# Expert weights of a one-core mixture-of-experts layer laid down with neighbouring rows on one partition

## The reference: what is computed

```python
pg = softmax(t @ wg + bg);  g = argmax(pg)              # one of 4 groups
le_g = (t @ we + be) restricted to group g              # 4 experts in it
v, idx = top_k(softmax(le_g), 2);  v = v / sum(v)
comb = one_hot weights p_top * v on the 16 experts
hg = einsum('td,edf->tef', t, w_gate)                   # w_gate: 16 x 1024 x 512
hu = einsum('td,edf->tef', t, w_up)                     # w_up:   16 x 1024 x 512
hid = silu(hg) * hu * comb
out = einsum('tef,efd->td', hid, w_down)                # w_down: 16 x 512 x 1024
x = layer_norm(ALPHA * x + g2 * out)
```

## Time and profile before

| | before |
|---|---|
| median of three runs | 502.61 us (501.02 to 505.34) |
| the profiled execution: time | 503.42 us |
| the profiled execution: span, first to last instruction | 501.4 us |
| what lies around the span | 2.0 us |
| mean granted TensorE clock | 0.962 |
| TensorE matmul busy | 439.5 us (88%) |
| DMA traffic | 147.16 MB, mean 293 GB/s |

### The profile page before, as it was taken

The page is one execution under the profiler, slowest core; times in us unless marked ns, Lnnn a source line. Parts: engine busy times, 40 slices in busy tenths (PEclk is TensorE's granted clock), DMA queues, the critical chain, the costliest instruction groups (busy, mean ns, idle before and its releaser), DMA issues.

```text
span 501.4 us, 6442 instructions
## 1 busy us (share of the span) xinstructions
PE 439.5 (88%) x2370; PEld 239.4 (48%) x2370; DVE 240.5 (48%) x439; ACT 120.8 (24%) x242; POOL 56.0 (11%) x58
## 2 busy tenths in 40 slices
PE   0777999999999998899999999999999998898500
PEld 0343555556554465794554355544445544553200
DVE  2651623847734257920122343444444444246797
ACT  2300158783220226251120111111111111220100
POOL 2000015357540340000000000000000000000000
PEclk9989899999999999899999999999999999999855
DMA  8999992855999045804999999999999999996003
GB/s 317 387 386 340 341 387 78 291 213 202 353 326 338 5 156 207 308 3 151 331 396 395 356 369 395 396 394 390 392 396 395 392 391 395 394 396 251 1 1 125
DMA packets 65011, 147.16 MB, mean 293 GB/s; under 512 B 3576, under 2 KB 4408, under 8 KB 64968
## 3 DMA queue, kind: packets, MB, share of 16 engines
q1 hardware_dynamic: 63776, 143.66, 77.7%
q10 hardware_dynamic: 1032, 2.81, 1.6%
q0 software_dynamic: 160, 0.10, 0.2%
HBM read 144.99 MB, written 1.58 MB: 292 GB/s over the span
## 4 chain that ended last, share of the span: by engine, by line
PE 77%; DVE 11%; DMA 5%; issue 4%; ACT 2%; SPq 0%; ACTq 0%; DVEq 0%
PE PS L1664 18%; PE PS L1432 12%; PE PS L1702 9%; PE PS L1533 8%; PE PS L1670 5%; PE PS L1363 4%; PE PS L1737 4%; DMA ring<-in_ex_w_gate 4%; PE PS L1608 4%; PE PS L1415 2%; PE PS L1709 1%; PE PS L1466 1%; PE PS L1744 1%; DMA rowB<-in_colsB 1%; PE PS L1684 1%
## 5 line engine op out<-in xcount | busy, mean ns | idle before, releaser
L1664 PE MATMUL PS<-ring,xs 128*64 128x256 f32 x896 | 102.9, 382 | 2.2 <-DMA ring<-in_ex_w_gate 1.7
L1664 PEld LDWEIGHTS PS<-ring,xs 128*64 128x64 f32 x896 | 61.9, 137 | 38.6 <-issue 10.1
L1432 PE MATMUL PS<-hT,ring 128*128 128x388 f32 x192 | 68.7, 511 | 3.9 <-DVE hT L849 3.9
L1702 PE MATMUL PS<-ring,hTs 128*64 128x512 f32 x224 | 52.9, 615 | 1.5 <-DMA ring<-in_ex_w_down 1.0
L1170 DVE SCALAR_TENSOR_TENSOR y<-PS,comb,y 128x1024 f32<-128x1024 f32 x42 | 53.5, 1278 | 0.3 <-PE PS L1744 0.3
L1432 PEld LDWEIGHTS PS<-hT,ring 128*128 128x128 f32 x192 | 37.7, 199 | 33.0 <-issue 7.7
L694 ACT CAST yh<-PS 128x512 fp32r<-128x512 f32 x14 | 8.2, 585 | 98.5 <-PE PS L1702 58.6
L1156 DVE TENSOR_TENSOR yl<-PS,yh 128x512 fp32r<-128x512 f32 x14 | 9.7, 691 | 44.6 <-ACT yh L694 44.6
L1702 PEld LDWEIGHTS PS<-ring,hTs 128*64 128x64 f32 x224 | 15.2, 140 | 31.8 <-issue 31.7
L1363 PE MATMUL PS<-ring,cond 128*32 128x512 f32 x192 | 24.9, 635 | 0.0
L1737 PE MATMUL PS<-yh,selT 64*128 64x512 f32 x84 | 20.8, 490 | 4.5 <-DVE y L1170 2.6
(11 more groups left out here) (256 smaller groups left out, 569.6 us busy)
## 6 DMA issues: line engine op xcount, KB each, us to landing
ring<-in_ex_w_gate SPq DMA_DIRECT2D x16, 2048.0 KB, 13.5
ring<-in_ex_w_up SPq DMA_DIRECT2D x16, 2048.0 KB, 15.9
ring<-in_ex_w_down SPq DMA_DIRECT2D x16, 2048.0 KB, 14.8
ring<-in_w_ada SPq DMA_DIRECT2D x12, 2048.0 KB, 14.4
ring<-in_w_in SPq DMA_DIRECT2D x3, 2048.0 KB, 20.5
ring<-in_w_out SPq DMA_DIRECT2D x2, 2048.0 KB, 10.4
xn<-in_x_sample SPq DMA_DIRECT2D x2, 512.0 KB, 6.3
pos<-in_pos SPq DMA_DIRECT2D x2, 512.0 KB, 7.2
```

Of the source, the lines that this page charges most:

```text
L1432: mm = pe.matmul(PS[:, w % 4, 0:W], wt[:, k, (w % 4) * P:(w % 4 + 1) * P], hT[:, k, :], start=(k == 0), stop=(k == KD - 1))
L1664: mm = pe.matmul(PS[HALF * h:HALF * (h + 1), j, 0:FE // 2], x(k, HALF), w[:, k, h * (FE // 2):(h + 1) * (FE // 2)], start=(k == 0), stop=( ...
L1702: mm = pe.matmul(PS[HALF * h:HALF * (h + 1), 3, :], x, w[:, f, h * 512:(h + 1) * 512], start=(f == 0), stop=(f == KF - 1))
```

## The change

The rows of an expert's matrices are dealt out differently. In gate and up units partition `p` now holds rows `8p` to `8p + 7`, which are neighbours in DRAM: one run of 16 KB. In down units it holds rows `2p, 2p + 1` of the first 256 and of the second 256: two runs of 8 KB. Chunk `k` of a gate or up unit is now every eighth feature, beginning with `k`, so `dispatch` takes every eighth column of `h2H` and `h2L` as its stationary operand (`chunk`, a step of 32 bytes), and `turn` takes every second hidden unit (`hid_chunk`, a step of 8 bytes). The matmuls of `project_in` and `project_out` are as before.

```diff
         experts = [
-            t["ex_w_gate"][0].rearrange("e (k p) n -> p e k n", p=P),
-            t["ex_w_up"][0].rearrange("e (k p) n -> p e k n", p=P),
-            t["ex_w_down"][0].rearrange("e (k p) n -> p e k n", p=P),
+            t["ex_w_gate"][0].rearrange("e (p k) n -> p e k n", p=P),
+            t["ex_w_up"][0].rearrange("e (p k) n -> p e k n", p=P),
+            t["ex_w_down"][0].rearrange("e (h p c) n -> p e h c n", h=2, p=P),
         ]
+        def expert_view(buf, j):
+            return buf[:, :].rearrange("p (h c n) -> p h c n", h=2, n=D) if j == 2 else unit3(buf)
+
+        def chunk(v, k):
+            return v.rearrange("p (q k) -> p k q", k=KD)[:, k, :]
+
+        def hid_chunk(f):
+            return hid[:, f // 2 * (FE // 2):(f // 2 + 1) * (FE // 2)].rearrange("p (q c) -> p c q", c=2)[:, f % 2, :]
...
-                sp.dma_start(weights(v, D if j == 2 else 512), experts[j][:, e]).then_inc(ring_in[v % SLOTS], 16)
+                sp.dma_start(expert_view(ring[v % SLOTS], j), experts[j][:, e]).then_inc(ring_in[v % SLOTS], 16)
...
-                        mm = pe.matmul(PS[:, 4 + n % 4, 0:HS], part[:, i, k * P:(k + 1) * P],
+                        mm = pe.matmul(PS[:, 4 + n % 4, 0:HS], chunk(part[:, i, :], k),
...
-                        mm = pe.transpose(PS[:, 2, c * P:(c + 1) * P], hid[:, c * P:(c + 1) * P], ident)
+                        mm = pe.transpose(PS[:, 2, c * P:(c + 1) * P], hid_chunk(c), ident)
```

More of the change, by code:

```diff
@@ L415, in again @@
                 for j in range(3):
-                    sp.dma_start(unit3(ring[j], D if j == 2 else 512),
-                                 experts[j][:, bass.ds(e, 1)].rearrange("p a k n -> p (a k) n")).then_inc(s["ov_in"], 16)
+                    w = experts[j][:, bass.ds(e, 1)]
+                    sp.dma_start(expert_view(ring[j], j),
+                                 w.rearrange("p a h c n -> p (a h) c n" if j == 2 else "p a k n -> p (a k) n"))\
+                        .then_inc(s["ov_in"], 16)
             overflow(sp, most, again)
```

## The result

The changed kernel takes **506.95 us** (median of 7 runs, 506.46 to 508.91) against 502.61 us, a ratio of **1.0096** with a 95% interval of 1.0073 to 1.0118. It is slower by 4.3 us, which the interval sets apart from no change. That is just under the 1% that the prediction took as what a measurement can tell, but outside its range (498.0 to 505.3 us) and on the other side of its forecast of 499.4 us.

A forecast was written before the change was run, and what follows sets the result against it. The prediction took TensorE to bound the expert stage, with 3.25 us of waits for weights to win back. With 0 for dispatch and transposes, 502.61 - 3.25 = 499.4 us; range 498.0 to 505.3 us.

The forecast's parts named there:

- What bounds the kernel: Expert stage: TensorE bounds it, its only waits for weights are four gaps from 411 to 428 us, 3.25 us.
- Part 1, the runs in DRAM: Expert transfers: longer pieces make an expert's transfer 3.6% to 7.3% faster and close all four waits: -3.25 us.
- The threshold of 2.5%: Expert transfers from 299 to 428 us: the speed-up needed to close all four waits, 3.25 / 129.
- Part 2, the dispatch: Line 1608: reading every eighth element as weights leaves the 173 ns pace unchanged, 0 us.
- rival A: Line 1608: doubled weight stream, load-bound at 219 ns, +4.0 to +5.0 us, 503.4 to 504.4 us; chance 0.29.
- the point named (207 ns pace): Dispatch: the pace from which the step costs more than the 3.25 us that the transfers give back.
- The cover of 70 ns: Dispatch: slack of the weight load, 173 - 103 ns, by which its stream may lengthen before the pace changes.
- the two readings given in the prediction: Dispatch, half the peak element rate: first, the moving side's peak, 499.4 us; second, the load's, 503.4 us or more.
- Part 3, the transposes: Line 1684, transposes of `hid`: a step of two elements costs 0, upper end 1 us.
- B: Dispatch: load costs much more, fourfold 522 us, or no longer overlaps (290 ns pace) 510.6 us; chance 0.07.
- C: Expert transfer isn't faster, 502.6 us (chance 0.09), or is slower, 560 to 590 us (chance 0.05).

The follow-up runs named there:

- r = 4: Changed kernel with gate and up units in runs of four rows (8 KB) and dispatch at a step of four elements: ratio 1.005, median 504.87 us.

## Why the prediction was wrong

**What bounds the kernel: right.** The stage is TensorE with gaps for weights at its end; nothing else that the intervals show came back when they closed, not even with half the bytes.

**Part 1, the runs in DRAM: right in mechanism and size.** 16 KB and 8 KB pieces move 423 to 425 GB/s from 360 to 411 us, where 409 is the rate of 4 KB; from 2 x 4.91 + 4.98 us an expert the prediction has 425. The waits went, and the rest turned into SyncE's waiting for buffers: 206 us of it from 225 us on with the new transfers alone, 194 before. The threshold of 2.5% lies between the 0.8% that left two waits and the 3 to 4% that left none. Only the 3.25 us were one execution's: another had 2.3 us, and the runs with the new transfers alone gain 0.7 to 2.8 us by their interval.

**Part 2, the dispatch: the step that failed.** "I take nothing, for one reason from the rows: the same engine reads its moving operand at 384 elements in 173 ns, 2.2 per ns, and weights at 1.25 per ns." That rate held for neighbours alone; at a step of eight the moving side reads 1.18 per ns. What came true is rival A's mechanism, a stream that becomes longer than its cover, at the place named and past the point named (207 ns pace). Its size was too small as well: 219 ns against 243 ns measured. The stream did not double, it grew by 150 ns, the difference of the records. The cover of 70 ns was nearly right: by it 188 + 70 = 258 ns is the longest record that the pace hides, and by the load-bound kernels, whose pace is the record less 95 ns, it is 173 + 95 = 268 ns (an estimate; no run has a record between 194 and 330 ns). That the matmuls at 1.2 GHz stay covered was right too: they take 320 ns with and without the step, which A's upper bound of 5.0 us didn't grant. So the miss in the sum is 6.1 us for the step, where 0 was taken and 4.0 to 5.0 were A's bounds, and with the transposes it is what carries the median past the range.

The Trainium skill's rule was the better guide. Its page "SBUF — State Buffer" (section "Door 1: The DMA port swizzle") wants two hits in each 16-byte line. The runs agree at a step of two elements (194 ns) and of eight (338 ns), and of the two readings given in the prediction the second is the nearer: a single hit for each line slows the load to 128 elements in 243 ns, and the moving side as well. They don't agree with its figure of four float32 elements as free, since at a step of four the load takes 330 ns. Nor do two hits make every load free: the transposes' went from 140 to 206 ns at a step of two. The runs show the threshold for the dispatch's loads; that lines of 16 bytes are its cause is not shown by them.

**Part 3, the transposes: small, and at the upper end.** The 140 ns loads became 206. Of the 0.13 us that the two transposes of a small expert have more, 0.08 us are paid, so about 1.1 us where 0 was taken and 1 was the upper end. The size of a step alone was no measure: a step of two costs a plain load 6 ns and a transpose's load 66 ns.

**The rivals.** A came true, 2.5 to 3.5 us above its own range of 503.4 to 504.4 us: 2.1 of them from the pace (24 ns x 87) and 1.1 from `hid`. Those 3.2 us fit; a gain from the transfers that is smaller over the runs than 3.25 us (by 1.5 us with the new transfers alone, by 0.3 us with half the bytes) is within the scatter of the medians. B's non-overlapping load (290 ns pace) and C didn't happen. The range failed because its upper end was put on A's own upper end with no room for A's size, although B's bound of 290 ns showed how far that size was open.

## What to carry to other kernels

Before a layout makes transfers longer, work out how much faster they need to be to close the waits that the trace shows; here 4 KB pieces were enough, and they cost the other side only a step of 8 bytes. Pay for a layout in the operand that is read with cover to spare: in the dispatch a float32 step of two elements was free under 384 moving columns, one of four or eight made weight loads the bound, and in the transposes of 128 columns already a step of two had a price. A rate that a trace shows for neighbouring elements says nothing about strided ones. And before a layout is judged by a difference of 2 or 3 us between two profiled executions, look for what else differs between them: where the dispatch began, and where TensorE was at 1.2 GHz.

## What the runs showed of the hardware

- Weight loads of 128 float32 columns have records of 188, 194, 330 and 338 ns at steps of 1, 2, 4 and 8 elements; at steps of 4 and 8 the dispatch is load-bound and paces at 95 ns less than its record (235 and 243 ns). At 1.2 GHz the matmuls with 384 columns take 320 ns at a step of 1 and of 8.
- A moving operand of 384 fp32r elements takes 173 ns as neighbours and 325 ns at a step of eight, at full clock.
- The weight load of a transpose is shorter (140 ns), but a step of two already costs it 66 ns.
- ScalarE's cast of 1024 elements, written at a step of 128, took 1.97 us, where the neighbouring write took about 1.04. VectorE's subtraction, which wrote and read one operand at that step, took 1.98 us in place of 1.22; what the write alone costs it is not shown.
- With one core, expert traffic from DRAM ran at 386 to 388 GB/s in 2 KB pieces and 409 in 4 KB. From 360 to 411 us it was 407 with all pieces of 4 KB, 419 with all of 8 KB (r = 4), and 423 to 424 with gate and up in 16 KB and down in 8 KB.
